# Token mixing of a two-layer streaming encoder: half swaps on ScalarE, weight low parts on VectorE, no replication product, and another step order

## What is computed

```python
def token_mix(z, pos, ...):                        # z = rmsnorm(h) @ w_in, 1824 columns
    u, va, q, k, vb, cq, ckv_raw, kpe_raw = split_proj(z)
    q = rope(q, pos); k = rope(k, pos)              # heads of 64: 8 query heads, 2 key heads
    qc = rmsnorm(cq, g_q) @ w_uq                    # 4 heads of 64 (nope) + 32 (rope)
    q_nope, q_pe = qc[..., :64], rope(qc[..., 64:], pos)
    kpe = rope(kpe_raw[:, :, None, :], pos)         # one shared key of 32, for all 4 heads
    a = chunk_mlp(u, va); b = sliding_window_attention(q, k, vb); c = latent_attention(...)
    return concat(a, b, c)                          # then h = h + concat @ w_out

def rope(x, pos):                                   # x1, x2: the halves of a head
    return concat([x1 * cos - x2 * sin, x2 * cos + x1 * sin])
```

## Time and profile before

| | us |
|---|---|
| median of three runs | 2052.89 |
| lowest and highest | 2052.47, 2054.03 |
| the profiled execution | 2052.6, its span 2050.8 |
| TensorE busy | 2026.9 (99% of the span) |
| VectorE busy | 1676.9 (82%) |
| ScalarE busy | 971.4 (47%) |
| GpSimd busy | 358.8 (17%) |
| TensorE's granted clock | 0.996 of full speed |

### The profile page before, as it was taken

The page is one execution under the profiler, slowest core; times in us unless marked ns, Lnnn a source line. Parts: engine busy times, 40 slices in busy tenths (PEclk is TensorE's granted clock), DMA queues, the critical chain, the costliest instruction groups (busy, mean ns, idle before and its releaser), DMA issues.

```text
span 2050.8 us, 41093 instructions
## 1 busy us (share of the span) xinstructions
PE 2026.9 (99%) x15433; PEld 1973.5 (96%) x15433; DVE 1676.9 (82%) x2481; ACT 971.4 (47%) x1749; POOL 358.8 (17%) x219
## 2 busy tenths in 40 slices
PE   9999999999999999999989999999999999999998
PEld 7999999999889999999989999999997899999998
DVE  6999998746667999998889999976457589999975
ACT  6544453334546544453455655433345464444532
POOL 1222200032112222200022222002321113222000
PEclk9999999999999999999999999999999999999999
DMA  4323233352122232232223322325321123232331
GB/s 134 100 85 102 83 91 94 84 132 67 35 54 84 85 100 91 93 93 81 75 85 101 102 82 80 113 78 118 89 65 53 44 83 100 85 102 79 97 94 65
DMA packets 236726, 178.34 MB, mean 87 GB/s; under 512 B 35808, under 2 KB 231616, under 8 KB 236608
## 3 DMA queue, kind: packets, MB, share of 16 engines
q1 hardware_dynamic: 234496, 174.62, 28.8%
q10 hardware_dynamic: 2112, 2.10, 0.3%
HBM read 170.12 MB, written 3.62 MB: 85 GB/s over the span
## 4 chain that ended last, share of the span: by engine, by line
PE 94%; DVE 2%; DMA 1%; issue 1%; ACT 1%; POOL 0%; SPq 0%; DVEq 0%; ACTq 0%
PE pair L1477 44%; PE pair L1424 30%; PE pair L1606 9%; PE pair L1533 4%; PE pair L1752 1%; PE pair L1731 1%; PE pair L1760 1%; PE pair L1743 1%; PE pair L1738 1%; PE pair L1775 1%; POOL w_low L853 0%; PE pair L1489 0%; DMA z_swapped<-z 0%; PE pair L1820 0%; DMA raw<-in_w_in_dram 0%
## 5 line engine op out<-in xcount | busy, mean ns | idle before, releaser
L1477 PE MATMUL pair<-t_parts,chunk_high 128*128 128x288 f32 x4592 | 919.3, 296 | 5.2 <-DVE t_parts L2071 2.2
L1477 PEld LDWEIGHTS pair<-t_parts,chunk_high 128*128 128x128 f32 x4592 | 739.1, 189 | 7.1 <-issue 3.8
L1477 PE MATMUL pair<-t_parts,chunk_low 128*128 128x288 f32 x2296 | 678.9, 296 | 0.0
L1477 PEld LDWEIGHTS pair<-t_parts,chunk_low 128*128 128x128 f32 x2296 | 432.6, 188 | 0.0
L859 POOL TENSOR_TENSOR chunk_low<-set_raw,chunk_high 128x512 fp32r<-128x512 f32 x164 | 237.3, 1457 | 866.5 <-ACT chunk_high L958 866.5
L958 ACT ACTIVATE chunk_high<-chunk_sum 128x512 fp32r<-128x512 f32 x328 | 204.3, 631 | 383.6 <-DVE chunk_sum L2029 189.2
L853 POOL TENSOR_TENSOR w_low<-raw,w_high 128x1024 fp32r<-128x1024 f32 (+2 forms) x48 | 113.9, 2377 | 618.6 <-ACT w_high L906 618.6
L2041 DVE TENSOR_TENSOR chunk_low<-chunk_sum,chunk_high 128x512 fp32r<-128x512 f32 x328 | 212.8, 690 | 8.3 <-ACT chunk_high L958 0.7
L1424 PE MATMUL pair<-hidden_high,w_high 128*128 128x288 f32 x896 | 192.0, 296 | 0.0
L1424 PE MATMUL pair<-hidden_high,w_low 128*128 128x288 f32 x896 | 191.9, 296 | 0.0
L1424 PE MATMUL pair<-hidden_low,w_high 128*128 128x288 f32 x896 | 191.6, 296 | 0.0
(11 more groups left out here) (295 smaller groups left out, 3698.6 us busy)
## 6 DMA issues: line engine op xcount, KB each, us to landing
set_raw<-in_w_up_dram SPq DMA_DIRECT2D x44, 1024.0 KB, 5.4
set_raw<-in_w_gate_dram SPq DMA_DIRECT2D x44, 1024.0 KB, 5.3
raw<-in_w_down_dram SPq DMA_DIRECT2D x64, 448.0 KB, 3.7
down_raw<-in_w_down_dram SPq DMA_DIRECT2D x16, 1024.0 KB, 5.4
raw<-in_w_in_dram SPq DMA_DIRECT2D x20, 512.0 KB, 4.2
raw<-in_w_in_dram SPq DMA_DIRECT2D x16, 256.0 KB, 3.8
raw<-in_w_out_dram SPq DMA_DIRECT2D x8, 512.0 KB, 3.5
raw<-in_w_out_dram SPq DMA_DIRECT2D x16, 256.0 KB, 4.0
```

The costliest lines, as they stand in the source:

```text
L1477: mm = nc.tensor.matmul(out, c[:, j, p, :], tr[p // 2][:, seat(p), x, t, :], start=p == 0 and n == 0, stop=p == KP - 1 and n == 2)
```

## The change

There are five parts, all inside the mixing of both layers.

1. **Half swap.** The four DMAs become four ScalarE copies of 32 partitions x 576, out of the PSUM pair of the product into `zr` (step `sw` now has four ScalarE operations). The division by the root mean square goes into the tables: `z:k` now scales cos64 and sin64, and z:k and z:q0 to q3 are not copied out of PSUM any more. `rot` reads the pair, and it is `rot:x.0` that frees it, behind the four copies.
2. **Shared key.** The weight tile of kpe is written four times side by side by the high part's copy (and by the low part), so that the product itself gives the replicated rows. `rep` falls away.
3. **`qp`'s weights** are loaded with the late tables (`d:in2` has six DMAs instead of three) and split in a step of their own, `uq`.
4. **Low parts** of the mixing's slots are made by VectorE, at steps `l:x` of the list, instead of by GpSimd. GpSimd keeps those of k and v.
5. **Order.** `PLAN` is another list, with other PSUM pairs.

```diff
-PLAN = """z:k@0 w:q0 d:q2 sumx@1 w:q1 d:q3 sw:k z:v@2 w:q2 d:va0 rot:k z:q0@0 tw@2 z:q1@1 w:q3 d:va1 sw:q1 rot:q1
-w:va0 d:u0 tc@2 w:va1 d:u1 sw:q0 ex:0 rot:q0 z:q2@0 z:q3@2 sw:q2 tv@0 rot:q2 w:u0 d:ckv sw:q3 S:0@1 E:0 z:va0@3 rot:q3
...
-B:7@1 w:C1""".split()
+PLAN = """w:q0 d:q2 z:k@0 d:q3 l:q0 sumx@1 d:va0 w:q1 w:q2 l:q1 sw:k z:v@2 rot:k l:q2 w:q3 z:q0@1 l:q3 d:va1 sw:q0
+z:q1@0 tw@2 rot:q0 d:u0 ex:0 w:va0 l:va0 d:u1 sw:q1 w:va1 rot:q1 z:q2@3 z:q3@1 sw:q2 l:va1 w:u0 sw:q3 tv@0 l:u0 rot:q2
...
+S:6@1 T:5@2 l:qn w:A0 l:A0 z:kpe@3 E:6 d:in2 sumq@2 qn:0@0 tckv@3 O:5@2 O:4@1 T:6@0 rot:kpe@3 d:B0 w:A1 rkv@1 S:7@2
+A:2@3 uq S:8@1 qn:1@0 E:7 qp@3 l:A1 vc:0@0 T:7@2 d:B1 rot:qp@3 E:8 kn:1@0 kn:0@2 S:9@1 O:6@0 T:8@2 A:0@3 E:9 A:5@2
...
+l:B3 ME:8 B:2@2 d:C1 MO:7@1 MO:6@3 MS:9@0 MT:8@1 ME:9 w:C0 B:5@2 MT:9@0 ex:1 l:C0 B:4@1 MO:9@2 MO:8@0 w:C1 l:C1 B:7@3
+B:6@0""".split()
@@ evacuated
+    if kind == "z" and arg in SWAPPED:
+        return [("vector", f"rot:{arg}.0")]
@@ late_tables
+                uq = a["mla_w_uq"][layer].rearrange("(k p) (h n) -> p k h n", p=P, n=C_NOPE + C_ROPE)
+                for k in range(KQ):
+                    sp.dma_start(uq_raw[:, k, :].rearrange("p (h n) -> p h n", h=C_HEADS), uq[:, k, :, C_NOPE:]).then_inc(mix_in, 16)
-            def half_swap(layer, z):
-
-                dve_did(sp, layer, f"z:{z}.0")
-                stand_alone(sp)
-                b = SWAPPED.index(z) % 2
-                for r in range(0, P, 32):
-                    sp.dma_start(zr[b][r:r + 32, :], zs[b][r ^ 32:(r ^ 32) + 32, :]).then_inc(swap_in[b], 16)
@@ GpSimd
-                for s in range(ZIN, F2D):
+                for s in range(ZIN, ZIN + 2):
                     low(layer, s, 0)
@@ ScalarE, high
+                if s == ZIN + WIN.index("kpe"):
+                    nc.scalar.activation(by_head(wh[s % RING]), four_times(s), ACT.Copy).then_inc(high_ready, 1)
+                    return
@@ ScalarE, mixing
+                    if kind == "sw":
+
+                        n = SWAPPED.index(arg)
+                        did("sumx" if n == 0 else f"z:{arg}")
+                        if n:
+                            dve_did(act, layer, f"rot:{SWAPPED[n - 2]}.2" if n > 1 else "z:k.1")
+                        for k, r in enumerate(range(0, P, 32)):
+                            copy(two(zr[n % 2][r:r + 32, :]), halves(PAIRS[f"z:{arg}"])[r ^ 32:(r ^ 32) + 32], f"{step}.{k}")
+                        continue
@@ TensorE
-                    elif kind == "rep":
-
-                        for half in range(2):
-                            mm = nc.tensor.matmul(ps[p][:, half, 0:HALF], rep32[:, :], zs[0][0:C_ROPE, half * HALF:(half + 1) * HALF], start=True, stop=True)
-                        mm = product(p, [(*tile_w(s, k, off), cqh[:, k, :], cql[:, k, :]) for k in range(KQ)])
+                        mm = product(p, [(uq_high[:, k, :], uq_low[:, k, :], cqh[:, k, :], cql[:, k, :]) for k in range(KQ)])
@@ VectorE, mixing
+                    if kind == "l":
+                        slot_low(layer, ZIN + MSLOTS.index(arg))
+                        continue
+                            dve.wait_ge(mix_in, layer * N_MIX_IN + MIX_IN_FIRST)
+                            emit(nc.vector.tensor_tensor(cos64[:, :], cos64[:, :], rms[:, :], ALU.mult), names[0])
+                            emit(nc.vector.tensor_tensor(sin64[:, :], sin64[:, :], rms[:, :], ALU.mult), names[1])
+                            continue
+                            own("z:k.1")
+                            adid(f"sw:{arg}.3")
+                            emit(nc.vector.tensor_tensor(rows2(dst), halves(PAIRS[f"z:{arg}"]), rows2(cos64), ALU.mult), names[0])
```

More of the change, by code:

```diff
@@ L172 @@
[L172 to L176, removed]
@@ L233, in vector_ops @@
     kind, arg = split(step)
-    n = {"z": 1, "sumx": 2, "sumq": 3, "tckv": 2, "tw": 1, "rot": 3, "a": 4, "qp": 1, "qn": 1,
+    n = {"z": 1, "sumx": 2, "sumq": 3, "tckv": 2, "tw": 1, "rot": 3, "a": 4, "qp": 1, "qn": 1, "uq": 1,
          "O": 1, "MO": 1, "A": 1, "B": 1, "E": 4, "ME": 2}.get(kind, 0)
@@ L324, in tensor_needs @@
     if prior is not None:
-        engine, name = evacuated(prior)
-        (scalar if engine == "scalar" else vector).append(name)
+        for engine, name in evacuated(prior):
+            (scalar if engine == "scalar" else vector).append(name)
     scalar += {
         "sumkv": lambda: ["z:ckv.0"],
-        "rot": lambda: ["rep.0"] if arg == "kpe" else [],
         "a": lambda: [f"tva:{arg}.1"],
@@ L341, in tensor_needs @@
         "sumq": lambda: ["z:cq2.2"],
-        "rot": lambda: [] if arg == "kpe" else ["qp.0"],
-        "rep": lambda: ["z:kpe.0"],
+        "rot": lambda: ["z:kpe.0"] if arg == "kpe" else ["qp.0"],
         "tv": lambda: ["z:v.0"],
@@ L1341, in mixing @@
                         tok_copies(step, va_tok[:, :, arg * P:(arg + 1) * P], P)
-                    elif kind == "rep":
-                        copy(two(kpe_rep[:, :]), halves(p), "rep.0")
                     elif kind == "kn":
@@ L1790, in c_part @@
                     if m < 4:
-                        engine, name = evacuated(last_in_pair(MIX, m))
-                        (act_did if engine == "scalar" else dve_did)(pe, layer, name)
+                        for engine, name in evacuated(last_in_pair(MIX, m)):
+                            (act_did if engine == "scalar" else dve_did)(pe, layer, name)
                     if m == 0:
@@ L2431, in mixing @@
                         own(DVE_STEPS[emitted[0] - 1])
-                    if kind not in ("sumx", "sumkv", "sumq", "tw", "rot", "E", "ME"):
+                    if kind not in ("sumx", "sumkv", "sumq", "tw", "rot", "E", "ME", "uq"):
                         pe_did(dve, layer, step)
@@ L2498, in mixing @@
                             continue
+                        src = {"kpe": kpe_rep, "qp": zs[1]}[arg]
+                        cos, sin = cos32, sin32
+                        if arg != "kpe":
+                            own("qp.0")
+                        else:
+                            own("z:kpe.0")
+                        if step == min(("rot:kpe", "rot:qp"), key=MIX.index):
+                            dve.wait_ge(mix_in, layer * N_MIX_IN + N_MIX_IN)
+                        emit(nc.vector.tensor_tensor(dst[:, :], src[:, :], cos[:, :], ALU.mult), names[0])
                         pe_did(dve, layer, step)
```

105 lines of the change are left out of this document (52 added, 53 removed).

## The result

The changed kernel takes **2059.89 us** (median of 7 runs, 2059.35 to 2063.34), the kernel before 2052.82 on the same chip. The ratio is 1.0038, with a 95% interval of 1.0028 to 1.0048. The change makes the kernel slower by 7.1 us; the forecast was slower by 3.1. Seven microseconds of 2053 are little, but in the traces they can be followed almost to the last one. The profiled execution of after took 2063.34 us, the slowest of the seven. A later one of the same code took 2060.01, so I use both.

A forecast was written before the change was run, and what follows sets the result against it. TensorE, busy 2026.9 of 2050.8 us, was taken as the bound. Waits adding 9.4 us less 6.3 removed gave +3.1, forecast 2056.0 us; own range 2053.8 to 2059.3, wide range 2049.5 to 2061.

The forecast's parts named there:

- The verdict I held likeliest: Whole kernel: time within about 0.2% (4.1 us) of before, counted as no change; chance 0.49.
- Removed: 6.3 us: TensorE in both mixings: `rep` 2.3 us, `tv` waits 3.1 and a wait of probability transposes 0.9 go.
- GpSimd's interference: Mixing: GpSimd's low parts stretch VectorE operations; taking this away is worth only 0.9 us in all.
- First wait: `z:q0` waits for q0's low part, queued on VectorE behind the reciprocal; 1.0 us a layer.
- Second wait: `z:q1` waits for pair 0, freed after q2's late load, its high part and the swap copies; 2.7 us a layer.
- Third wait: First product of `c_part` waits for pair 0 until VectorE adds `B:6` into h; 1.0 us a layer.
- Moved loads: `rot:kpe` waits for six `d:in2` DMAs, hidden by six steps; no wait taken, upper end 0.35 us a layer.
- Fed without a gap: Rival: the new list leaves TensorE no waits in the mixings, only the 6.3 us saving counts; 2046.6 us, chance 0.14.
- The load doesn't bind: Rival: q2 lands early or copies are cheap, so 5.4 us of waiting before `z:q1` vanish; 2050.6 us, chance 0.12.
- VectorE becomes late in attention: Rival: low parts delay VectorE's queue from `MS:0` to `B:6`, adding 5.4 us; 2061.4 us, chance 0.16.

The follow-up runs named there:

- mended kernel: The changed kernel with q0's low part listed ahead of `z:k` and `B:6` moved from PSUM pair 0 to pair 2; 2046.34 us, ratio to before 0.9968.
- filled kernel: The changed kernel with throwaway TensorE matmuls: 20 ahead of `z:q1` (2059.74 us), or 8 ahead of `z:q0` and 20 ahead of `z:q1` (2059.76 us).

## Why the prediction was right, and where it fell short

The forecast was 2056.0 us and the result 2059.9. That is inside the wide range (2049.5 to 2061) and 0.6 us above the forecast's own, which ended at 2059.3. The sign and the three waits of the forecast were right, but the kernel lost 7.1 us where 3.1 were forecast. The verdict I held likeliest, within 0.2%, is not what came; slower by more than 0.2% had 0.36.

**Removed: 6.3 us. The number right, by luck.** With all waits gone, the mixings take 441.15 us against 447.54 before, 6.4 less, and the timer says 2046.34 against 2052.75, 6.4 less as well. But two errors cancel in it. The prediction read layer 1 as like layer 0, at the full clock, and there the clock fell and cost 1.5 us. By the start times of TensorE's matmuls, the products (`product`, every 128x288 matmul of one) take 6.3 us less in the mended kernel than before: 4.0 of listed waits, 1.5 of clock, and 0.8 for four streams stopped and started. With the 2.3 of `rep` that makes 8.6. Against it the other matmuls of the mixings take 1.05 us more in each layer from start to start, 2.1 in all, mostly the transposes of probabilities and the scores (0.67 and 0.45 in layer 0). The prediction had no term for that, and no run tests why the new order makes them longer.

**GpSimd's interference: 0.9 us. Right for the order before, and not a general price.** In the mended list the same low parts on GpSimd cost 3.5 us of the mixings, 2.7 of them listed waits, and 4.0 by the timer. How much a blocking costs depends on what it meets. The operation of 2.06 us in the earlier trace rows did not end with GpSimd's low part, as the prediction has it, but 0.62 us after it (463.73 against 463.11).

**First wait: 1.0 us a layer. Mechanism right, size nearly.** The waits were 1.5 and 1.0 (2.1 in all in the later execution). The missing 0.5 is the landing of the tables, which I had priced only for q2's load and not for the scaling of the cosines.

**Second wait: 2.7 us a layer. Right, partly because two errors cancel.** The waits were 2.6 and 3.0. The copies took 2.64 and not 2.3, since they did not overlap. The load took 4.6 us from issue to copy in layer 0, where I had 4.8, and 5.0 in layer 1. The Trainium skill's budget (ScalarE: Activation LUTs, Rules for kernel authors) had given 3.1 us for the four copies and 3.5 for the wait. The measured copies lie between it and mine, and both waits below its 3.5.

**Third wait: 1.0 us a layer. Right,** 0.96 in the chain.

**Moved loads: 0, up to 0.35 a layer.** They were late once, by 0.3 us. Right within the bound for this kernel; with other orders and fillers they were up to 0.8 us late in a layer.

**The step that failed** is the one with which the sum was made: "Two layers x (1.0 + 2.7 + 1.0) = 9.4 added". It takes the length of a wait for what the wait costs, and the 6.3 removed do the same. Two things come on top.
- The matmul stream's end and start: 0.23 us at the third wait, and 6.65 against 6.4 for a product that stands behind one. Seven waits make about 1.7 us.
- The clock: behind the second wait `z:q1` ran partly at the lower level, 1.4 and 1.2 us in the profiled execution of after.

The waits by the list, 10.3, with 1.7 and 2.6 make 14.6 us. The mixings of after are 455.99 - 441.15 = 14.8 us longer than those without waits. That closes the account in the trace: 14.8 - 6.4 = 8.4 us over before, where the clock's part in before (1.5 us) is inside the 6.4.

**What stays open** is the timer's side of the clock. The changed kernel is 7.1 and 7.8 us slower than before by its two medians, which fits 8.4. But filled so that the clock stays up, it is still 7.2 and 7.9 us slower, where the trace of the filled kernel has mixings only 5.8 to 6.1 us longer than before. The stretches outside the mixings differ by 1 to 2 us between executions (from the start to `sumx` 414.0 to 415.8 us, between the mixings 786.2 to 788.0), and five runs don't average that away. Part of that is the clock again, between the mixings: in eight traces (before's and the changed kernel's later one among them) it falls there for two short stretches and the part takes 786.2 to 786.4 us, in five it falls once for twice as long and the part takes 787.4 to 787.7, and in one both stretches are long and it takes 788.0. The fall behind the second wait is shown in all four traces of the three kernels that have it unfilled at 2.5 us or more; that it puts 2.6 us into the timed median is not shown.

**The rivals.** "Fed without a gap" was false for this list and true one step away from it: the steps had the margins that I had found, all but the three. "The load doesn't bind" was false. "VectorE becomes late in attention" was false: no entry on it there, so the argument that GpSimd's blockings leave the same queue held.

## What to carry to other kernels

Lay a new order out engine by engine and look at the few places where a queue stands behind something slow: one low part placed behind a 3.75 us reciprocal held back a load, a high part and four copies, and cost 10 of the 13.5 us that this list loses. When TensorE is the bound, charge a wait more than its length: about 0.25 us for stopping the stream, and in this case 1.2 to 2.6 us of lower clock behind each wait of 2.5 us or more and behind one of 1.8. Count this also for the waits that a change removes, and read every layer of the kernel before, not one. When a bank pair is to be changed, look at its last user as well as at its next.

## What the runs showed of the hardware

- **The clock behind a wait.** In a mixing where TensorE was otherwise busy, but for one wait of about 1 us in some, the granted clock fell behind every wait of 2.5 to 3.5 us that was seen (2.5, 2.5, 2.6, 2.7, 2.9, 2.9, 3.0 and 3.5). It also fell behind one of the two `tv` waits of before, that of 1.8 us, and stayed at 1.00 behind the other, of 1.3. It stayed at 1.00 behind 0.9, 1.0, 1.3, 2.1 and 2.3 us in the other kernels. So the length of a wait alone doesn't decide it between 1.8 and 2.3 us, and what does is open. It came with the next product's first matmul or up to 1.4 us into it, and the low stretch was 3.0 to 5.5 us long. The Trainium skill (TensorE: Matmul & The Clock Gate, HAM oscillation — how this bites in real kernels) describes waits for transfers after which the next burst starts cold. These traces agree that a transfer's wait can do it, here once in a layer and not only in a loop.
- **A copy of a quarter of the partitions costs a whole one.** 32x576 out of PSUM took 0.66 us on ScalarE, like the 0.65 of 128x576, and four in a row 2.64. At this width a quarter of the partitions saved nothing.
- **GpSimd beside VectorE.** A VectorE operation with both inputs in SBUF went from 0.69 to 2.87 us beside a GpSimd operation of 2.41 us, more than the 2.06 of the earlier trace rows.
